# Expert token rows fetched by an indexed DMA, bias rows as row-group products, the down bias applied once by the gates, and a nine-slot weight ring in a mixture-of-experts decoder step

## What is computed

```python
h = rmsnorm(x, norm2_g)
top_v, top_i = lax.top_k(h @ w_router + b_router, 4)
gates = softmax(top_v)
gu = h[rows of e] @ w_gate_up[e] + b_gate_up[e]        # 1024 -> 2048
gate, up = min(gu[:, :1024], 7), clip(gu[:, 1024:], -7, 7)
y_e = ((up + 1) * gate * sigmoid(1.702 * gate)) @ w_down[e] + b_down[e]
x = x + sum over the 4 experts of gates * y_e;   y = rmsnorm(x, final_norm_g)
```

## Time and profile before

| | us |
|---|---|
| median of 3 runs | 1442.11 (1436.14 to 1444.95) |
| the profiled execution: its span, first to last instruction | 1444.9 |
| ahead of pair 0's first product | 365 |
| sixteen pairs, to the last add | 1067 |
| final norm and stores | 13 |

### The profile page before, as it was taken

How to read it: one execution, slowest core, us unless ns; L and a number is a source line. 1 busy time by engine, 2 the same in 40 slices (tenths; PEclk the granted TensorE clock), 3 DMA queues, 4 the chain that set the end, 5 groups by cost and what they waited for, 6 DMA issues and landing times.

```text
span 1444.9 us, 15673 instructions
## 1 busy us (share of the span) xinstructions
PE 1394.6 (97%) x6385; PEld 652.2 (45%) x6385; DVE 312.6 (22%) x575; ACT 196.6 (14%) x333; POOL 84.6 (6%) x110
## 2 busy tenths in 40 slices
PE   6999999997999999999999999999999999999996
PEld 4757667645343443434343434434343434343432
DVE  2434365622021111111111112111111111111112
ACT  1134321210110101010101011110101011011101
POOL 4267200000000000000000000000000000000000
PEclk9999999996899998889999999998888999999987
DMA  9247450645668999999999999999998999999992
GB/s 313 85 147 235 129 197 0 252 149 215 238 243 339 369 371 369 373 369 371 390 354 374 363 377 400 403 390 374 370 373 369 372 389 388 376 367 373 367 375 84
DMA packets 92154, 447.61 MB, mean 310 GB/s; under 512 B 6298, under 2 KB 15942, under 8 KB 59221
## 3 DMA queue, kind: packets, MB, share of 16 engines
q1 hardware_dynamic: 85447, 427.35, 74.7%
q0 software_dynamic: 5632, 18.88, 4.2%
q10 hardware_dynamic: 1046, 0.97, 0.2%
HBM read 445.73 MB, written 1.68 MB: 310 GB/s over the span
## 4 chain that ended last, share of the span: by engine, by line
PE 94%; DVE 3%; ACT 1%; issue 1%; DMA 0%; ACTq 0%; DVEq 0%; SPq 0%
PE ps L949 33%; PE ps L997 17%; PE ps L910 10%; PE ps L960 5%; PE ps L786 4%; PE ps L970 2%; PE ps L759 2%; PE ps L1009 2%; PE ps L615 2%; PE ps L976 2%; DVE arena L1629 1%; PE ps L1017 1%; PE ps L502 1%; PE ps L633 1%; PE ps L1013 1%; PE ps L548 1%
## 5 line engine op out<-in xcount | busy, mean ns | idle before, releaser
L949 PE MATMUL ps<-arena 128*64 128x512 f32 x2048 | 481.2, 629 | 4.5 <-DVE arena L1629 4.4
L949 PEld LDWEIGHTS ps<-arena 128*64 128x64 f32 x2048 | 169.6, 145 | 312.6 <-issue 294.3
L997 PE MATMUL ps<-arena 128*64 128x512 f32 x1024 | 246.0, 642 | 1.5 <-ACT arena L1041 1.5
L1041 ACT ACTIVATE arena<-ps 128x512 f32<-128x512 f32 (+9 forms) x169 | 95.5, 583 | 515.1 <-PE ps L997 225.7
L997 PEld LDWEIGHTS ps<-arena 128*64 128x64 f32 x1024 | 76.8, 148 | 161.4 <-issue 155.1
L910 PE MATMUL ps<-arena 128*128 128x128 f32 (+1 forms) x768 | 142.7, 318 | 1.1 <-DVE arena L1591 1.1
L910 PEld LDWEIGHTS ps<-arena 128*128 128x128 f32 (+1 forms) x768 | 109.0, 195 | 44.0 <-issue 15.5
L1611 DVE TENSOR_SCALAR arena<-ps 128x512 f32<-128x512 f32 x32 | 22.1, 692 | 474.5 <-PE ps L949 474.5
L1212 ACT ACTIVATE arena<-arena 128x512 f32<-128x512 f32 x32 | 20.2, 631 | 507.6 <-DVE arena L1611 507.6
L1626 DVE TENSOR_TENSOR arena<-arena,ps 64x512 f32<-64x512 f32 x16 | 10.9, 679 | 282.3 <-PE ps L1013 282.3
L960 PE MATMUL ps<-arena 2*128 2x512 f32 x128 | 69.8, 690 | 0.0
(11 more groups left out here) (282 smaller groups left out, 881.1 us busy)
## 6 DMA issues: line engine op xcount, KB each, us to landing
arena<-in_w_gate_up SPq DMA_DIRECT2D x128, 2048.0 KB, 11.9
arena<-in_w_down SPq DMA_DIRECT2D x64, 2048.0 KB, 12.3
arena<-in_w_in SPq DMA_DIRECT2D x8, 1024.0 KB, 9.3
arena<-in_w_out SPq DMA_DIRECT2D x2, 2048.0 KB, 11.7
arena<-in_w_in SPq DMA_DIRECT2D x2, 1088.0 KB, 11.9
arena<-in_w_in SPq DMA_DIRECT2D x1, 2048.0 KB, 23.8
arena<-in_consts SPq DMA_DIRECT2D x1, 1096.0 KB, 7.8
arena<-in_w_uq SPq DMA_DIRECT2D x1, 768.0 KB, 15.0
```

The source lines that it names most:

```text
L949: m = mm(ps[SL * e:SL * e + SL, b, :], xg[:, 2 * c + kk, SL * e:SL * e + SL], w[e][:, kk, b, :], start=(c == 0 and kk == 0), stop=(c == 3 ...
L997: m = mm(ps[SL * e:SL * e + SL, u, :], hidT[:, 4 * c + kk, SL * e:SL * e + SL], w[e][:, kk, u, :], start=False, stop=(c == 1 and kk == 3), ...
L1041: return act.activation(out, in_, ACT.Copy)
```

## The change

- **Rows by DMA.** The normed rows are written to a DRAM tensor `h2_rows` (three transfers from ACT's queue). For a pair, TensorE transposes `pickg` (`turn_pick`); VectorE finds, for each of the 128 slots, the token with the largest entry (`max`, then `max_index`: `find_slots`); GpSimd issues an indexed DMA that fetches those 128 rows of 4 KB into `rows_in` (`gather`); TensorE turns them with eight transposes (`turn_rows`), ScalarE copies them to one of two `xg`. The indices of pair n+2 are found and the rows of pair n+1 are turned while pair n is between its gate/up and its down products. The products of `gather` (L910) go.
- **Bias.** `b_gate_up` lies in rows 0, 32, 64 and 96 (four quarters of 512) of one of two buffers, and its four products use four different row groups of the array; the down bias products in each pair go, and `gates x b_down` is added once, in pair 0, by six products.
- **Ring.** Nine slots instead of six, over all pairs, with the chunk number modulo nine (`where`). The DRAM arrays `w_gate_up` and `w_down` are laid out on the host so that a chunk is 2 MiB in one piece, 16 KB for a partition.
- **Order and banks.** The down products' first half begins before the second half of `hid` is transposed; the results to tokens use banks 4 to 7 and 2; the adds to `x` come in halves. All pairs are written out on all engines, and `final_g` is loaded at the end into the ring. Several semaphores are merged.

```diff
+        ring = slot[0:4] + [spare[0], spare[2], slot[4], slot[5], spare[1]]
+        NR = len(ring)
+        h2_rows = nc.dram_tensor("h2_rows", (T, D), F32, kind="Internal").ap()
+        def where(n, c):
+            q = CHUNKS * n + c
+            return q % NR, q // NR
...
-                sp.dma_start(dst.rearrange("p (k n) -> p k n", k=count),
-                             rows[:, bass.ds((2 * p + c % 2) * KD + k, count), :]).then_inc(signal, 16)
+                sp.dma_start(ring[s], rows[bass.ds(of, 1), :, :].rearrange("o p n -> p (o n)")).then_inc(in_chunk[s], 16)
...
+            def gather():
+                off = bass.IndirectOffsetOnAxis(ap=slot_tok[:, 0:1], axis=0)
+                pool.indirect_dma_start(rows_in, None, h2_rows, off).then_inc(in_rows, 16)
+            pool.wait_ge(h2_out, 48)
+            for n in range(NP):
+                pool.wait_ge(slot_known, n + 1)
+                if n:
+                    pool.wait_ge(pe_xgT, n)
+                gather()
...
+            def turn_rows(n):
+                pe.wait_ge(in_rows, 16 * n + 16)
                 for k in range(KD):
-                    for t in range(NT):
-                        n = ROWS[t]
-                        m = mm(ps[:, 6 + k // 4, P * (k % 4):P * (k % 4) + P], h2[0:n, t, P * k:P * k + P],
-                               pick[0:n, t, :, :].rearrange("p u s -> p (u s)"), start=(t == 0), stop=(t == NT - 1))
+                    m = nc.tensor.transpose(ps[:, 6 + k // 4, P * (k % 4):P * (k % 4) + P],
+                                            rows_in[:, P * k:P * k + P], ident)
+                m.then_inc(pe_xgT, 1)
...
-                            row = b_gate if b < 2 else b_up
-                            mm(ps[:, b, :], half[1], row[:, 512 * (b % 2):512 * (b % 2) + 512], start=False,
-                               stop=False, skip_group_check=True)
+                            m = mm(ps[:, b, :], half[b], buf[32 * b:32 * b + 2, :], start=False, stop=False,
+                                   skip_group_check=True)
...
+                for j in range(4):
+                    m = nc.tensor.transpose(ps[:, 4, P * j:P * j + P], hid[:, P * j:P * j + P], ident)
+                m.then_inc(pe_hidT, 1)
+                if ahead > 1:
+                    turn_pick(n + 2, 5)
+                if ahead > 0:
+                    turn_rows(n + 1)
...
+            def find_slots(n, src, more=False):
+                dve.wait_ge(pickT_ready, n + 1)
+                dve.max(best8, src).then_inc(best_ready, 1)
+                dve.wait_ge(best_ready, n + 1)
+                if n is not first_pair:
+                    dve.wait_ge(in_rows, 16 * n)
+                dve.max_index(slot_tok, best8, src).then_inc(slot_known, 1)
...
+        if name == "w_gate_up":
+            v = v.reshape(NE, 4, 2, P, 2 * D).transpose(0, 1, 3, 2, 4).reshape(NE, 4, P, SLOT)
```

More of the change, by code:

```diff
@@ L364, in _ @@
[L364 to L385, removed]
+            def load_chunk(p, c, s):
+                rows, of = ((gu_rows, (2 * p + c % 2) * 4 + c // 2) if c < 8 else
+                            (dn_rows, (2 * p + c % 2) * 2 + c // 2 - 4))
+                sp.dma_start(ring[s], rows[bass.ds(of, 1), :, :].rearrange("o p n -> p (o n)")).then_inc(in_chunk[s], 16)
@@ L962, in pair @@
-                if ahead:
-                    pe.wait_ge(pickT_ready, n + 1)
-                    pe.wait_ge(y_added, 3 * n + 1)
-                    gather(n + 2)
-                pe.wait_ge(gate_ready, 2 * n + 2)
-                pe.wait_ge(in_b_down, 16 * n + 16)
-                for u in range(2):
-                    mm(ps[:, u, :], half[2], b_down[:, 512 * u:512 * u + 512], start=True, stop=False,
-                       skip_group_check=True)
-                pe.wait_ge(y_added, 3 * n + 3)
@@ new lines, in pair, with down @@
+                        m.then_inc(pe_bias, 1)
+                if not first:
+                    pe.wait_ge(y_added, 5 * n)
+                pe.wait_ge(hid_ready, 2 * n + 1)
+                for j in range(4):
[5 more added lines that the diff above has]
+                    turn_rows(n + 1)
+                def down(c, steps):
+                    for j, (kk, u) in steps:
+                        for e in range(2):
+                            m = mm(ps[SL * e:SL * e + SL, u, :], hidT[:, 4 * c + kk, SL * e:SL * e + SL],
+                                   w[e][:, kk, u, :], start=(c == 0 and kk == 0), stop=(c == 1 and kk == 3),
+                                   skip_group_check=True)
+                            if j == 7:
+                                m.then_inc(ring_free[places[8 + 2 * c + e][0]], 1)
+                        if c == 1 and j == 3:
+                            m.then_inc(pe_down, 1)
@@ L1015, in pair @@
-                m.then_inc(pe_comb, 1)
-                for t in range(2):
-                    m = mm(ps[:, 3 + 2 * t, :], pickT[:, t, :], ye[:, 512:D], start=True, stop=True)
-                    m.then_inc(pe_comb, 1)
-            gather(1)
-            pair(0, False, True, first=True)
-            with pe.Fori(1, NP - 1) as p:
-                pair(p, False, True)
-            pair(NP - 1, False, False)
+                        s, before = places[8 + 2 * c + e]
+                        pe.wait_ge(in_chunk[s], 16 * before + 16)
@@ new lines, in _ @@
+            turn_pick(0, 4)
+            for t, rows in enumerate(turned):
+                m = nc.tensor.transpose(ps[0:NE, 3, P * t:P * t + rows], gates[0:rows, t, :], ident[0:rows, 0:rows])
+            turn_pick(1, 2)
+            pe.wait_ge(gT_ready, 1)
+            turn_rows(0)
+            pe.wait_ge(pickT_ready, 2)
+            for n in range(NP):
+                pair(n, [where(n, c) for c in range(CHUNKS)], min(2, NP - 1 - n), xg[n % 2], pickT[n % 3],
+                     in_bias[n % 2], 32 * (n // 2) + 32, first=(n == 0))
@@ L1029, in _ @@
                     with pe.Fori(0, NP) as p:
-                        pair(j * NP + p + NP, True, False)
+                        n = j * NP + p + NP
+                        pe.wait_ge(y_added, 5 * n)
+                        turn_pick(n, 5)
+                        turn_rows(n)
+                        pair(n, [where_more(j * NP + p, c) for c in range(CHUNKS)], 0, xg[0], pickT[0],
+                             in_bias[0], 32 * (j * NP + p) + 16 * NP + 32)
             pe.wait_ge(y_final, 1)
@@ L1634, in _ @@
-            dve.sem_inc(y_added, 3)
-            choose(slice(0, 2), 1, slice(0, SL))
+                    add(x[:, t, 0:512], ps[:, 4 + 2 * t, :], t + 1)
+                add(y_last, ps[0:64, 2, :], 3)
+                for t in range(2):
+                    add(x[:, t, 512:D], ps[:, 5 + 2 * t, :], t + 4)
+            first_pair = 0
+            choose(slice(0, 2), 0, slice(0, SL))
+            find_slots(0, pickT[0])
+            dve.wait_ge(pe_pick, 1)
+            choose(slice(2, 4), 1, slice(0, SL))
```

453 lines of the change are left out of this document (260 added, 193 removed).

## The result

| us | before | after |
|---|---|---|
| median (lowest to highest; four runs each) | 1439.12 (1429.67 to 1444.95) | 1318.76 (1314.12 to 1321.75) |
| profiled execution, its span | 1444.9 | 1318.3 |
| up to pair 0's first product | 365 | 360.2 |
| sixteen pairs, to the last products | 1065 | 944.7 |
| from there to the end | 14 | 13.4 |

The ratio is 0.9193, 95% interval 0.915 to 0.9236; 1324 was predicted. Nearly all of the gain lies in the pairs: 66.6 us each before, 944.7 / 16 = 59.0 after.

What follows compares the result with a forecast made beforehand. TensorE set the pace before; after, the DMA engines at 61 us a pair. Restart at 369, chunks 909.4, gathers 18.8 and 29 behind make 1326, predicted as 1324 us; own range 1303 to 1346, 8 in 10 1303 to 1372.

Steps and rivals of the forecast that it cites:

- TensorE, 50.6 us a pair: TensorE's work in a pair after the change, against 62.5 us before; 53.4 us at worst.
- The bias: Gate/up bias products in four row groups: 0.9 us a pair if all four run at once, against 3.70.
- The six down-bias products of pair 0: The `gates x b_down` products in pair 0: 3 us, lying under the stream.
- DMA, 61 us a pair at 422 and 391 GB/s: Transfers of a pair: 59.6 us for weight chunks plus 1.3 us for gathered rows; the bound moves to the DMA engines.
- The 372 GB/s that stand there for rows of 1 KB: DMA rate at a full share for rows of 1 KB, read from a window as 387 / 1.04.
- rival A: Expert weight stream: longer rows give no rate, it runs at 402 GB/s; 1372 us, or 1369 as a median; chance 0.11.
- The ring: Nine chunk slots keep the DMA engines at a full share: two being read, seven landing or waiting, 35 us of transfers.
- Rival D: Whole expert part: a stream without pauses runs slower than its bursts, at 368 GB/s; 1461 us; chance 0.03.
- Rival B: Pairs: TensorE stays the bound at a lower clock, mean 0.80, deciding below 0.83; 1387 us; chance 0.11.
- C: Pairs: a DMA share of 0.98 is already the engines' end, each pair takes 63.8 plus 1.3 us; 1416; chance 0.04.
- Start and end: Pair 0 begins at 360 us, 5 us won or 4 lost; 29 us follow the last chunk's landing.
- The three parts of the sum: Stream restarts at 369 us; chunks 909.4 and gathers 18.8 us, last landing at 1297; 29 us behind it; 1326.

## Why the prediction was right, point by point

**TensorE, 50.6 us a pair:** 50.30 in pair 1 at PEclk 1.00. The bias was 1.14 us instead of 0.9, 3.2 times faster than 3.70; the 3.07 times of the Trainium skill (TensorE: Matmul & The Clock Gate, Measured speedup vs the span model) was the nearer figure, and the trace agrees with it. The six down-bias products of pair 0 were mis-sized: back to tokens took 12.3 us there (408.56 to 420.88) instead of 4.9, so 7.4 and not 3. The head start covered that: from 400 to 420.9 us the DMA share is 1.01 at 426 GB/s.

**DMA, 61 us a pair at 422 and 391 GB/s:** 60.2 at 427, gathers included. Two terms were off, both to the dear side: the rate by 1%, and the gather, 0.9 us and not 1.3. The 372 GB/s that stand there for rows of 1 KB are a misreading that no term of the sum rests on: in that window lie the second half of `w_out` (rows of 2 KB), the router's weights (rows of 128 B) and the first chunks (8 KB). The step from which I took rival A was wrong as well: 394 / 0.98 is not what rows of 4 and 8 KB can do. Unbroken they run at 417, so A, had it been true, would have been 1337 and not 1369.

**The ring:** nine slots did let the DMA engines stay at a full share, but that was not their worth: with six the rate is 427 GB/s as well. The three more brought the head start of 16 us; the full rate came with PE no longer being late.

**Rival D** fell: 426 GB/s over 915 us without a break. The Trainium skill's 358 GB/s (DMA: Bandwidth & Descriptors, Where 436 GB/s comes from) doesn't hold in this trace; the 425 of its HBM Reference, Specifications (TRN2), does.

**Rival B** fell too, though PE waits in every pair from pair 3 on: PEclk was 0.96 and not under 0.83. No wait was longer than 3.0 us, and 10 of the 26 of 2 us or more had no slow stretch right behind them. **C** fell with the full share of 1.01.

**Start and end.** PE's timeline of after at the start of pair 0 and in the last pair, as the earlier trace rows:

```profile
357.09 1.94 PE L959 MATMUL ps<-arena 128*128 128x128 f32 x8 [3.87 <-DMA arena<-h_rows,arena]
360.19 10.00 PE L980 MATMUL ps<-arena 128*64 128x512 f32 x32 [1.16 <-issue]
...
1290.92 9.12 PE L1008 MATMUL ps<-arena 128*64 128x512 f32 x40
1299.98 1.98 PE L1048 MATMUL ps<-arena 128*128 128x512 f32 x4
1301.89 1.05 PE L1056 MATMUL ps<-arena 128*32 128x512 f32 x4
1302.87 1.99 PE L1048 MATMUL ps<-arena 128*128 128x512 f32 x4
```

Pair 0 began at 360.19 (predicted 360; in the second profiled execution of the same kernel at 356.75, so an agreement this close is luck), with 3.87 us of waiting for the first rows, the only place where anyone waits for a gather; its first block took 10.0 us instead of 9.13. The three parts of the sum, predicted and measured: restart at 369 and 371.5; stream 928.2 and 920.5, to the last bytes at about 1292; tail 29 and 26.3, because the last 32 down records ran mostly at 2.4 GHz. 1326 against 1318.3: the miss of 7.7 us is the stream's, the start and the tail nearly cancel.

**What the gain is not.** PE's work fell from about 62.5 to 50.3 us a pair, and the stretches at 1.2 GHz behind two-row products went; of these 16 us a pair 7.6 came out as time (66.6 to 59.0). The rest is mostly PE's wait for chunks now. What remains to be had in the pairs lies in bytes and rate, not in products.

## What to carry to other kernels

Where a second engine stands close behind the bound, price a change as the longer of the two after it, and then ask what moves the new bound: here either of two cuts in PE's work gave over three quarters of the gain, and the layout, worth nothing that could be measured before, gave about 19 us after. A wait in a queue that follows the bound (SP's for slots) is no proof that its resource is short. Rows that nobody uses, once the transfers are the bound, are worth leaving out.

## What the runs showed of the hardware that I had not expected

Products with only two rows count as busy in the profile, and yet PEclk falls from 1.00 to 0.60 (changed kernel, one row group) or 0.51 (kernel before) with or right behind 3.7 us of them, and the block behind is slow in 16 of 16 pairs of the one and 13 of 16 of the other. With four row groups at once (1.14 us) and 48 idle products, where PE never waits, PEclk is 1.00. Waits of up to 3 us did less: 51 of them leave PEclk at 0.96 to 0.97. The rate of one core's stream grew with the length of its rows: 348 GB/s at 1 KB (`w_in`, 188 to 192 us of before: 1372 packets, 1.39 MB), 417 at 4 and 8 KB, 427 at 16 KB; only the last step was tried with all else the same. At its end the stream thins out: over the last 5.5 us the mean share is 0.60, which fits engines that finish one after another, but no view shows them singly. And 128x128 products of the same matrix with itself took 0.114 us a record against the gather's 0.179; why was not looked into.
